# First normalisation of a hybrid decoder trunk: where the transposed rows of the next chunks are copied

## The reference

```python
def rmsnorm(x, g):
    xf = x.astype(jnp.float32)
    y = xf * lax.rsqrt(jnp.mean(xf * xf, axis=-1, keepdims=True) + EPS)
    return (y * g.astype(jnp.float32)).astype(x.dtype)

def rglru_block(xn, h0, conv_buf, w_in, ...):
    u = xn @ w_in
    gate, xb = u[..., :D_RNN], u[..., D_RNN:]
    xc, new_buf = causal_dwconv(xb, conv_buf, conv_w, conv_b)
    ...
y, h_i, c_i = rglru_block(rmsnorm(x, P['a_norm'][i]), ...)
```

## Time and profile before

| | us |
|---|---|
| median of 3 runs (2483.46 to 2483.73) | 2483.58 |
| the profiled execution | 2483.79 |
| its span | 2481.9 |
| TensorE busy in it | 2459.2 |
| VectorE busy | 1235.3 |
| ScalarE busy | 773.5 |
| GpSimd busy | 277.1 |

### The profile page before, as it was taken

The page is one execution under the profiler, slowest core; times in us unless marked ns, Lnnn a source line. Parts: engine busy times, 40 slices in busy tenths (PEclk is TensorE's granted clock), DMA queues, the critical chain, the costliest instruction groups (busy, mean ns, idle before and its releaser), DMA issues.

```text
span 2481.9 us, 39879 instructions
## 1 busy us (share of the span) xinstructions
PE 2459.2 (99%) x15287; PEld 2404.6 (97%) x15287; DVE 1235.3 (50%) x2004; ACT 773.5 (31%) x1266; POOL 277.1 (11%) x395
## 2 busy tenths in 40 slices
PE   8999999999999999999999999999999999999999
PEld 7999999999999999999999868999999999999999
DVE  7666645533542543444556585355335425434542
ACT  6554532212311321112344585332113212211221
POOL 3212620000000000001220253200000000000000
PEclk9999999999999999999999999999999999999999
DMA  4111111111111111111372203111111111111112
GB/s 127 43 51 43 43 43 51 38 38 51 43 40 53 42 40 44 51 42 38 110 138 57 70 2 107 43 43 41 43 51 42 40 53 42 38 46 51 42 36 92
DMA packets 227189, 130.95 MB, mean 53 GB/s; under 512 B 24789, under 2 KB 224669, under 8 KB 226876
## 3 DMA queue, kind: packets, MB, share of 16 engines
q1 hardware_dynamic: 224948, 126.47, 17.5%
q10 hardware_dynamic: 2100, 3.37, 1.1%
q0 software_dynamic: 64, 0.05, 0.0%
HBM read 116.76 MB, written 15.01 MB: 53 GB/s over the span
## 4 chain that ended last, share of the span: by engine, by line
PE 97%; DVE 1%; ACT 1%; issue 1%; POOL 0%; DMA 0%; POOLq 0%; DVEq 0%; ACTq 0%
PE ps L876 30%; PE ps L878 30%; PE ps L877 30%; PE ps L1295 1%; PE ps L1271 1%; PE ps L1243 1%; PE ps L1166 0%; PE ps L1343 0%; PE ps L1345 0%; PE ps L1344 0%; PE ps L1159 0%; PE ps L1064 0%; PE ps L863 0%; PE ps L1045 0%; PE ps L1177 0%
## 5 line engine op out<-in xcount | busy, mean ns | idle before, releaser
L876 PE MATMUL ps<-sa,whi 128*128 128x384 f32 (+1 forms) x1836 | 600.1, 327 | 0.0
L878 PE MATMUL ps<-sa,wlo 128*128 128x384 f32 (+1 forms) x1836 | 599.2, 326 | 0.0
L877 PE MATMUL ps<-sa,whi 128*128 128x384 f32 (+1 forms) x1836 | 598.7, 326 | 0.0
L876 PE MATMUL ps<-sb,whi 128*128 128x384 f32 (+1 forms) x1764 | 581.8, 330 | 0.0
L878 PE MATMUL ps<-sb,wlo 128*128 128x384 f32 (+1 forms) x1764 | 575.7, 326 | 0.0
L877 PE MATMUL ps<-sb,whi 128*128 128x384 f32 (+1 forms) x1764 | 575.2, 326 | 0.0
L1405 ACT ACTIVATE whi<-raw 128x1024 fp32r<-128x1024 f32 (+1 forms) x204 | 201.4, 987 | 873.3 <-PE ps L878 855.4
L876 PEld LDWEIGHTS ps<-sa,whi 128*128 128x128 f32 x1836 | 344.6, 188 | 1.0 <-issue 0.3
L877 PEld LDWEIGHTS ps<-sa,whi 128*128 128x128 f32 x1836 | 344.6, 188 | 0.3
L878 PEld LDWEIGHTS ps<-sa,wlo 128*128 128x128 f32 x1836 | 344.6, 188 | 0.0
L876 PEld LDWEIGHTS ps<-sb,whi 128*128 128x128 f32 x1764 | 331.3, 188 | 2.8 <-issue 1.2
(11 more groups left out here) (359 smaller groups left out, 2558.6 us busy)
## 6 DMA issues: line engine op xcount, KB each, us to landing
raw<-in_f_w_up SPq DMA_DIRECT2D x96, 512.0 KB, 3.8
raw<-in_f_w_down SPq DMA_DIRECT2D x64, 384.0 KB, 3.4
raw<-in_a_w_in SPq DMA_DIRECT2D x16, 512.0 KB, 3.9
x_spill<-x SPq DMA_DIRECT2D x1, 4352.0 KB, 15.0
x<-x_spill SPq DMA_DIRECT2D x8, 544.0 KB, 6.0
xrows<-in_x_prompt SPq DMA_DIRECT2D x8, 512.0 KB, 6.6
raw<-in_a_w_out SPq DMA_DIRECT2D x8, 512.0 KB, 4.1
raw<-in_w_q SPq DMA_DIRECT2D x16, 256.0 KB, 3.6
```

Of the source, the lines that this page charges most:

```text
L876: pe.matmul(out, whi[s][:, w], mhi[k][:, chunk(c)], start=(k == 0), stop=False)
L877: pe.matmul(out, whi[s][:, w], mlo[k][:, chunk(c)], start=False, stop=False)
L878: last = pe.matmul(out, wlo[s][:, w], mhi[k][:, chunk(c)], start=False, stop=(k == nk - 1))
```

## The change

It moves work within the first 45 us and adds 12 transposes.

- TensorE first makes `N_WARM` = 12 transposes of the identity into bank 7, which nobody reads.
- Jobs 10 and 11 (token row tile 5), which stood ahead of piece (0,0), now stand in piece (0,1) behind two steps; jobs 12 and 13 in the same piece behind six steps; jobs 14 and 15 in piece (1,0) behind two steps; jobs 16 and 17, which stood ahead of piece (1,0), behind it. Job 12 goes to bank 5 in place of 1.
- On VectorE and ScalarE the copies of jobs 6 to 11 leave the steps of chunk 0 and stand behind its last one. On VectorE two of the three stand ahead of the second weight split and the third behind it; on ScalarE all three stand behind the weight conversion.
- The copies of jobs 12 to 17 stand behind other steps of chunk 1; the last ones behind its last step. On ScalarE job 2's copy stands behind the third square and the roots.
- SyncE issues the first weight load behind a wait for token row 0, and the second one behind token rows 3 to 5.

```diff
-        SET_BANK = [0, 1, 2, 3, 4, 5] + [1, 2, 4, 5, 1, 2] + [1, 4, 2, 5, 2, 5] + [7, 7, 6, 7]
+        SET_BANK = [0, 1, 2, 3, 4, 5] + [1, 2, 4, 5, 1, 2] + [5, 4, 2, 5, 2, 5] + [7, 7, 6, 7]
+        N_WARM = 12
...
-            conv_loads(0)
-            for tt in range(3, 9):
+            eng.wait_ge(rows_in[0], 16)
+            conv_loads(0, (0,))
+            for tt in range(3, 6):
+                token_rows(tt)
+            conv_loads(0, (1,))
+            for tt in range(6, 9):
                 token_rows(tt)
...
             def first_products():
 
+                for _ in range(N_WARM):
+                    pe.transpose(ps[:, 7, 0:P], ident[:, :], ident[:, :])
                 set_up(0, SET_END[0])
                 pe.wait_ge(an_in, 16)
                 pe.transpose(ps[:, 7, 0:KD], anrow[:, :], ident[0:KD, 0:KD]).then_inc(an_tr, 1)
                 root_spread(0)
-                set_up(SET_END[0], SET_END[1])
+                set_up(SET_END[0], SET_END[1] - 2)
+
+                def ready(c, k):
+                    if (c, k) == (1, 2):
+                        set_up(SET_END[1] + 2, SET_END[1] + 4)
+                    elif (c, k) == (1, KD - 2):
+                        root_spread(2)
+                    normed(0)(c, k)
+
+                def transposes(c, k):
+                    if (c, k) == (0, 2):
+                        set_up(SET_END[1] - 2, SET_END[1])
+                    elif (c, k) == (0, KD - 2):
+                        set_up(SET_END[1], SET_END[1] + 2)
+
                 for c in range(3):
                     for s in range(2):
                         if c == 0:
                             pe.wait_ge(hi_ready[s], 1)
                             pe.wait_ge(lo_ready[s], 1)
                         if s == 0:
-                            pe.wait_ge(tr_act, SET_END[c] // 2 + (c == 1))
-                            pe.wait_ge(tr_dve, SET_END[c] // 2 + (c == 1))
...
-                        piece(0, s, c, KD, split_a, None if s else ready)
+                            pe.wait_ge(tr_act, SET_END[c] // 2)
+                            pe.wait_ge(tr_dve, SET_END[c] // 2)
+                        elif c == 1:
+                            pe.wait_ge(tr_dve, SET_END[1] // 2 + 1)
+                        piece(0, s, c, KD, split_a, transposes if s else ready)
                         if (c, s) == (0, 0):
                             root_spread(1)
-                            set_up(SET_END[1], SET_END[2] - 2)
-                        elif (c, s) == (0, 1):
-                            set_up(SET_END[2] - 2, SET_END[2])
+                        elif (c, s) == (1, 0):
+                            set_up(SET_END[1] + 4, SET_END[2])
...
             row_squares(0)
             set_up(0, 1)
             row_squares(1)
-            set_up(2, 3)
             row_squares(2)
             row_roots(0)
+            set_up(2, 3)
             set_up(4, 5)
             prep(0, 0, KD * P)
 
             def first_chunk_in(k):
                 if k in (1, 3, 5):
                     row_squares((k - 1) // 2 + 3)
-                elif k in (2, 4, 6):
-                    set_up(SET_END[0] + k - 2, SET_END[0] + k - 1)
-                if k == 6:
+                elif k == 6:
                     row_roots(1)
                 elif k == 7:
                     prep(0, 1, KD * P)
+                    set_up(SET_END[0], SET_END[1])
...
-                elif k in (1, 3, 5):
-                    set_up(SET_END[1] + k - 1, SET_END[1] + k)
+                elif k in (1, 5):
+                    set_up(SET_END[1] + (k - 1) // 2, SET_END[1] + (k - 1) // 2 + 1)
+                elif k == 7:
+                    set_up(SET_END[1] + 4, SET_END[2])
...
                 if k == 0:
                     prep(0, 0, KD * P)
-                elif k in (3, 4, 5):
-                    set_up(SET_END[0] + 2 * (k - 3), SET_END[0] + 2 * (k - 3) + 2)
                 elif k == 7:
                     row_inverse(1)
+                    set_up(SET_END[0], SET_END[0] + 4)
                     prep(0, 1, KD * P)
+                    set_up(SET_END[0] + 4, SET_END[1])
 
             def second_chunk_in(k):
-                if k in (1, 3, 6):
-                    m = SET_END[1] + 2 * (1, 3, 6).index(k)
-                    set_up(m, m + 2)
+                if k == 2:
+                    set_up(SET_END[1], SET_END[1] + 2)
                 elif k == 5:
                     row_inverse(2)
+                elif k == 6:
+                    set_up(SET_END[1] + 2, SET_END[1] + 4)
+                elif k == 7:
+                    set_up(SET_END[1] + 4, SET_END[2])
```

More of the change, by code:

```diff
@@ L634, in gate_load, with conv_loads @@
                     eng.dma_start(dst, gate_w(w, c, m)).then_inc(raw_ready[s], 16)
-            def conv_loads(c):
-                for s in range(2):
+            def conv_loads(c, slots=(0, 1)):
+                for s in slots:
                     load(4 * c, s, w_cols(w_in, D + c * 256 + s * P), KD * P)
@@ L952, in first_products @@
                         if s == 0:
-                            pe.wait_ge(tr_act, SET_END[c] // 2 + (c == 1))
-                            pe.wait_ge(tr_dve, SET_END[c] // 2 + (c == 1))
-                        def ready(c, k):
-                            if (c, k) == (1, KD - 2):
-                                root_spread(2)
-                            normed(0)(c, k)
-                        piece(0, s, c, KD, split_a, None if s else ready)
+                            pe.wait_ge(tr_act, SET_END[c] // 2)
[3 more added lines that the diff above has]
+                        piece(0, s, c, KD, split_a, transposes if s else ready)
                         if (c, s) == (0, 0):
                             root_spread(1)
-                            set_up(SET_END[1], SET_END[2] - 2)
-                        elif (c, s) == (0, 1):
-                            set_up(SET_END[2] - 2, SET_END[2])
+                        elif (c, s) == (1, 0):
+                            set_up(SET_END[1] + 4, SET_END[2])
                         elif (c, s) == (1, 1):
```

## The result

| | before | changed |
|---|---|---|
| median, us | 2483.58 | 2489.92 |
| range of 13 runs each, us | 2483.18 to 2484.59 | 2488.22 to 2491.88 |
| profiled execution: its time, its span, us | 2483.79, 2481.9 | 2489.92, 2488.0 |
| mean granted clock of TensorE | 0.997 | 0.996 |

The ratio is 1.0024, 95% interval 1.0017 to 1.0031: slower by a quarter of a per cent, where 2485.2 (2482.4 to 2487.6) was forecast.

The account below looks back on a forecast made before the run. It took TensorE, hanging in the start on the normalisation chains of chunks 0 and 1, as the bound. Terms +1.1 - 0.1 + 0.6 = +1.6 us gave 2485.4 for the profiled execution, 2485.2 us median, range 2482.4 to 2487.6.

Parts of the forecast that it names:

- Warm transposes, ScalarE's order, loads: Start: earlier transposes and third square bring VectorE's first multiplication from 10.84 to about 10.6, -0.25 us; loads cost 0.
- Chunk 0's chain: Normalisation of chunk 0: with three copies gone, VectorE's last subtraction moves from 20.06 to 18.6 us.
- The new wait: Copy 11 on VectorE waits for transposes inside (0,1): chunk 1's normalisation starts at 24.5 instead of 23.40, +1.1 us.
- Chunk 1 and the requests' transposes: Chunk 1: sixth operand at 33.5 (-0.1 term); requests' transposes behind (1,0) add 0.6; (1,1) starts 1.6 us later.
- Chunk 2, hidden: Chunk 2's normalisation starts 3.1 us later, nearly hidden by ScalarE's wait; (2,0) ends 1.6 us later, 0.2 us left.
- The step that failed: After the first pair's six pieces, start gains or losses reach the end one for one; twelve early transposes cost nothing.
- Rival C, the clock: Start or behind the 285.5 us pause: TensorE's low-clock stretch shortens or lengthens, -2.6 to +2.6 us; chance 0.15.
- Rivals A: TensorE's head start in (1,0) counts: 2482.0, milder 2484.1 us; chance 0.2 for 2482.0 to 2484.3.
- B: First weights land late, at 11.3 us, shifting the chain by 1.3: 2486.5 us, up to 2487.8; chance 0.1.
- D: The change does nothing to the end, both chains being held by something misread: 2483.6 us; within A's 0.2.

Follow-up runs that it names:

- e5: Changed kernel with ScalarE's 3 MB write moved behind the query-weight load and the transposes of jobs 10 and 11 back ahead of piece (0,1): 2484.78 us.
- e6: Changed kernel with the 3 MB write behind the query-weight load and the requests' transposes inside (1,0), ahead of its sixth step: 2485.52 us.
- e3: Kernel before with only the twelve early transposes of the identity added: 2486.31 us, ratio 1.0011.
- e4: Changed kernel without the twelve early transposes of the identity: 2489.97 us.
- e1: Changed kernel with only ScalarE's 3 MB write moved behind the landing of the query-weight load: 2486.45 us, ratio 1.0012.
- e15: Changed kernel with the 3 MB write behind the query-weight load and 28 identity transposes in TensorE's pause at 287 us: 2485.25 us.
- e17: Changed kernel again, unaltered, for a second profile: 2491.29 us, ratio 1.0030.
- e7: Kernel before with two other banks for deferred copies, later jobs inside (0,1) and (1,0), the change's load order and the late 3 MB write: 2483.06 us.
- e10: e7 with 28 identity transposes added in TensorE's pause at 285 us: 2481.23 us, ratio 0.9988.
- e9: Kernel before with only 28 identity transposes added in TensorE's 3.50 us pause at 285.5 us: median 2486.07 us.
- e12: Changed kernel with the edits of e1, e5 and e6 and 28 identity transposes in the pause at 285 us: 2482.66 us, ratio 0.9994.
- e13: Changed kernel with 28 identity transposes in the pause at 287 us, its 3 MB write untouched: 2484.53 us, ratio 1.0000.
- e14: e15 with two identity transposes ahead of each of steps 2 to 6 of (0,0) and twelve ahead of (1,0)'s sixth step: 2483.55 us.
- e16: e10 with the twelve early identity transposes added at its start: 2479.87 us, ratio 0.9982.

## Why the prediction was wrong, point by point

- **Warm transposes, ScalarE's order, loads: -0.25.** The first multiplication came at 10.24 (forecast 10.6), the weights landed 8.7 us into the span (9.3). Transposes of real rows have a median of 273 ns already between 4.4 and 7.2 us, where the earlier trace rows have 421. Right in sign, but less than half of the 0.60 us that this execution shows (10.84 to 10.24); some of that is the scatter of single executions.
- **Chunk 0's chain.** Last subtraction 18.25 (18.6), weight subtraction 19.98 (20.4), first matmuls of (0,0) and (0,1) at 13.31 and 21.34 (13.6 and 21.6). Right.
- **The new wait.** Copy 11 waited, and chunk 1 began at 24.43 (24.5). e5 takes it out and gets 1.08 us. The core of the forecast held, with some luck in the number: from the first multiplication to (1,1) the change added 2.34 us (24.40 to 26.74) where the forecast had 1.85, and the larger gain ahead of it made up for that.
- **Chunk 1 and the requests' transposes.** Sixth step at 33.55 with a 1.63 us wait (33.5, over 1.5), (1,1) at 36.98 (36.8 to 36.9), e6 worth 0.51 (0.6). Right.
- **Chunk 2, hidden.** ScalarE waited 1.04 us before the parameter copy at 41.83. Right; the spare time was 1.0 us, not 0.2.
- **The step that failed** is the sentence that from the start on "anything gained or lost arrives at the end one for one", and under it the twelve transposes at "no cost". What they cost comes 1250 us later. With the 24 instructions more, SyncE's issue of a load takes 1029 ns instead of 583 and the load lands 33.1 us behind it instead of 28.2, beside a 3 MB write. TensorE pauses for 2.9 us and its clock falls for 3.4, together 4.7 us. That the twelve alone bring it (e3), that it goes without them (e4) and that it goes when the write is moved (e1) is shown; that it works by the instruction fetch is the reading that fits all 19 executions, and stays open. I had looked for other pauses only among those of the trace of before, and a load that lands 1.7 us ahead of its use makes no pause there. I asked of the start's loads how many microseconds they had in hand, and of none behind it.
- **Rival C, the clock,** had its place wrong. It was sought in the start and at 285 us; in the profiled execution the fall, 1.57 us, stands behind the new pause. But e1, e4 and e15 show that the fall in the first pieces is real too, and the clock moves more than the 2.6 us I allowed: six of e4's ten runs lie some 5 us above the other four, with a mean granted clock of 0.994 to 0.996 against 0.996 to 0.998. In e4's profiled execution, one of the six, the low stretches last 23.9 us in all, of which 6.8 are in the first pieces; before it is 13.7. Rivals A, B and D did not come: (1,0) got its sixth operand at 33.5, and the first weights came in time.

By the forecast's own terms, 2485.2 plus 3.15 for the pause and 1.57 for the clock is 2489.9, the measured median. That it fits to a tenth is luck: the start was 0.15 us dearer in the profiled execution, the low stretches behind 1400 us took 0.4 off, and the changed kernel again (e17) has a median of 2491.29.

## What to carry to other kernels

Before an edit is costed at nothing because it stands in idle time, list the transfers and conversions of the whole program with little time in hand, and above all the small loads that are issued beside a large one on another queue: added instructions can move such a race that shares nothing else with them. A large write that nobody awaits soon should be issued behind the loads that somebody does await. Where an engine must pause for some microseconds, filling the pause with harmless work can be worth more than the work around it: here 28 transposes kept the clock and took 1.8 us off (e7 to e10), about as much as the change had cost in the start. And before a gain of a microsecond is put down to an edit, the low stretches of both profiles should be set side by side: each of 3.41 us was worth 1.1 to 1.6 us here, and they come and go far from the edit.

## What the runs showed of the hardware

- Two queues with work for the same DMA engines passed equal numbers of packets (267 and 265 in 4 us), so the load of 256-byte packets got 0.07 MB where the 3 MB write of 1536-byte packets got 0.41. But behind the write's first packets the load had stood still for 3.8 to 5.1 us, or for 12.1 to 14.4 when its issue had taken over 1000 ns.
- An instruction fetch recorded up to 0.3 us ahead of one issue of SyncE goes with 1029 to 1706 ns for the next issue, a fetch elsewhere with 583 to 587: 10 and 9 of 19 executions.
- A stretch of 3.41 us at TensorE's lower level cost 1.57 us. Such stretches followed a pause of 1.6 us in pieces that had been broken before (e1, 33.74), and one of 2.9 us in a dense stretch; 28 transposes of 128x128 in a pause of 3.5 us prevented it in e9, e10, e12, e13, e14, e15 and e16.
- Transposes alone bring TensorE to its upper level: in the kernel before it was there at 7.6 us with no matmul ahead of it. In the 13 profiled executions with twelve or more transposes from about 1.6 us on, it was there at 4.3 to 7.2 us (5.7 in the changed kernel), in the six without them at 7.6 to 10.1. The latest is e9, whose first 24 transposes took 5.36 us instead of 4.23.
